# A two-model forward pass on one core: the forget-log sums of the recurrent mixer, with stacked parts and another order

## The reference, cut to what matters

```
q, f, i, g, u = split(rmsnorm(x) @ w_in)
log_f = logaddexp(log(lb), log1p(-lb) + log_sigmoid(f))   # forget logs, (token, channel)
k = (1 - lb) * sigmoid(-f);  v = i
S_t = diag(exp(log_f_t)) S_{t-1} + k_t (outer) v_t
o_t = S_t^T q_t
o = o * rsqrt(mean(o*o) + eps) * norm_g * silu(g)
```

## Time and profile before

| | |
|---|---|
| median of 3 runs | 2926.18 us (2925.79 to 2926.19) |
| the profiled execution's own time | 2925.35 us |
| its span, first to last instruction | 2923.6 us |
| PE busy | 2892.8 us, 99% |
| DVE busy | 2029.5 us, 69% |
| ACT busy | 1297.4 us, 44% |
| POOL busy | 575.4 us, 20% |
| mean granted TensorE clock | 0.998 |

### The profile page before, as it was taken

How to read it: one execution, slowest core, us unless ns; L and a number is a source line. 1 busy time by engine, 2 the same in 40 slices (tenths; PEclk the granted TensorE clock), 3 DMA queues, 4 the chain that set the end, 5 groups by cost and what they waited for, 6 DMA issues and landing times.

```text
span 2923.6 us, 40420 instructions
## 1 busy us (share of the span) xinstructions
PE 2892.8 (99%) x16738; PEld 2501.0 (86%) x16738; DVE 2029.5 (69%) x2542; ACT 1297.4 (44%) x1619; POOL 575.4 (20%) x380
## 2 busy tenths in 40 slices
PE   8999999999999999999999999999999999999998
PEld 6786877868899988888889998899988888889997
DVE  5656556565788884575668887788874665678887
ACT  5545445354534335434543333443346434443332
POOL 0000000000344310200033441343400200034431
PEclk9999999999999999999999999999999999999999
DMA  4121221212233232113222222322332123222222
GB/s 162 44 87 51 101 87 44 89 61 89 99 119 106 101 114 105 35 64 134 91 87 101 101 102 101 108 101 92 111 110 101 43 73 130 80 93 102 101 102 73
DMA packets 41959, 270.10 MB, mean 92 GB/s; under 512 B 5776, under 2 KB 6032, under 8 KB 10672
## 3 DMA queue, kind: packets, MB, share of 16 engines
q1 hardware_dynamic: 41776, 267.52, 25.8%
HBM read 265.33 MB, written 2.10 MB: 91 GB/s over the span
## 4 chain that ended last, share of the span: by engine, by line
PE 89%; DVE 6%; ACT 3%; issue 1%; DVEq 1%; DMA 0%; POOL 0%; SPq 0%; ACTq 0%; POOLq 0%
PE PS L313 27%; PE PS L315 26%; PE PS L314 26%; PE PS L691 1%; PE PS L2426 1%; PE PS L1211 1%; DVE w_lo L287 1%; PE PS L1239 1%; ACT w_hi L279 1%; DVE XT L1724 1%; DVEq L1697 1%; PE PS L750 1%; PE PS L1052 0%; DVE ff_a L1711 0%; PE PS L2406 0%
## 5 line engine op out<-in xcount | busy, mean ns | idle before, releaser
L287 DVE TENSOR_TENSOR w_lo<-w_raw,w_hi 128x2048 fp32r<-128x2048 f32 x167 | 382.6, 2291 | 308.5 <-ACT w_hi L279 307.2
L279 ACT ACTIVATE w_hi<-w_raw 128x2048 fp32r<-128x2048 f32 x169 | 323.2, 1912 | 419.4 <-PE PS L315 419.2
L313 PE MATMUL PS<-uh_b,w_hi 128*128 128x256 f32 (+1 forms) x1096 | 358.9, 327 | 0.0
L315 PE MATMUL PS<-uh_b,w_lo 128*128 128x256 f32 (+1 forms) x1096 | 357.9, 327 | 0.0
L314 PE MATMUL PS<-ul_b,w_hi 128*128 128x256 f32 (+1 forms) x1096 | 357.7, 326 | 0.0
L209 ACT ACTIVATE w_hi<-w_raw 128x1536 fp32r<-128x1536 f32 x72 | 107.3, 1491 | 477.8 <-PE PS L315 477.8
L313 PE MATMUL PS<-uh_a,w_hi 128*128 128x512 f32 (+1 forms) x792 | 288.7, 364 | 1.1 <-DVE ul_a L639 0.7
L314 PE MATMUL PS<-ul_a,w_hi 128*128 128x512 f32 (+1 forms) x792 | 285.5, 360 | 0.0
L315 PE MATMUL PS<-uh_a,w_lo 128*128 128x512 f32 (+1 forms) x792 | 285.5, 360 | 0.0
L313 PE MATMUL PS<-ff_h_hi,w_hi 128*128 128x512 f32 x704 | 278.4, 395 | 5.0 <-DVE XT L1724 4.5
L314 PE MATMUL PS<-ff_h_lo,w_hi 128*128 128x512 f32 x704 | 274.5, 390 | 0.0
(11 more groups left out here) (400 smaller groups left out, 6549.5 us busy)
## 6 DMA issues: line engine op xcount, KB each, us to landing
w_raw<-in_weights SPq DMA_DIRECT2D x241, 1024.0 KB, 4.8
XT<-in_xT SPq DMA_DIRECT2D x8, 256.0 KB, 6.1
mem_raw<-in_mem SPq DMA_DIRECT2D x2, 1024.0 KB, 5.4
out<-XT SPq DMA_DIRECT2D x8, 256.0 KB, 2.0
bands<-in_bands SPq DMA_DIRECT2D x2, 768.0 KB, 6.3
w_raw<-in_weights SPq DMA_DIRECT2D x4, 256.0 KB, 4.7
p_raw<-in_pT SPq DMA_DIRECT2D x2, 512.0 KB, 3.8
lb<-in_lb_logits SPq DMA_DIRECT2D x2, 512.0 KB, 5.7
```

The lines of the kernel that those rows point to most:

```text
L279: act.activation(self.hi[g % 2][:], self.raw[g % 2][:], ACT.Copy).then_inc(self.hi_done.sem, 1)
L287: dve.tensor_tensor(self.lo[g % 2][:], self.raw[g % 2][:], self.hi[g % 2][:], ALU.subtract).then_inc(self.lo_done.sem, 1)
L313: pe.matmul(out, sh, mh, start=first, stop=False, skip_group_check=onto)
L315: return pe.matmul(out, sl, mh, start=False, stop=last, skip_group_check=onto)
```

## The change: what it does

The two parts of the forget logs are no longer two products over 128 tokens. The table `level` has a property: the columns of the tile's first 64 tokens need only logs of the first 64 tokens; those of the last 64 tokens need only logs of the last 64, but for the eighth group, which also needs the sum of all the first 64. So a stationary operand is built for each half of the tile: 64 partitions with the `hi` parts of its 64 tokens and 64 with their `lo` parts. `early` (in `m.LFhi`) is that of the first half, `late` (in `u[1]`) that of the second. The tables are stacked alike. `sums` becomes three matmuls: `late` over 512 columns, `early` over 64 columns of ones, and `early` over 512 columns.

The operands are made in other places: ACT copies half the partitions in the projection (same free size), DVE subtracts into the other half there. After the projection ACT copies the second half's `hi` parts in two pieces (between the table `after` and the queries), and DVE makes their `lo` parts in two pieces. ACT also copies 64 columns of ones. ACT's exponent writes to `m.E` in runs of 64 elements in place of 128. `decays` takes its ones from another tile and now stands between head 0's second and third sums.

```diff
@@ PoolAndStates.scalar
         k.w.wait_used(act, self.proj.g0 + 9)
-        act.activation(uh[:, 6, 0:P], m.after, ACT.Copy).then_inc(self.tables_hi.sem, 1)
+        act.activation(uh[:, 6, 2 * P:2 * P + HALFP], k.ones[:].to_broadcast([P, HALFP]), ACT.Copy)
+        act.activation(uh[:, 6, 0:2 * P], m.after, ACT.Copy).then_inc(self.tables_hi.sem, 1)
+        for a in (0, 2):
+            act.activation(self.u[1][HALFP:P, a:a + 2, :], m.LF[HALFP:P, a:a + 2, :], ACT.Copy).then_inc(self.proj.lf_hi.sem, 1)
         for h in range(HH):
             act.activation(m.Q[:, h, :], k.PS[:, 4 + h, :], ACT.Copy).then_inc(self.proj.qread.sem, 1)
@@ MixerProjection.scalar and .vector
-        act.activation(m.LFhi[:, :, 0:DA], m.LF[:], ACT.Copy).then_inc(self.lf_hi.sem, 1)
+        act.activation(m.LFhi[0:HALFP, :, 0:DA], m.LF[0:HALFP], ACT.Copy).then_inc(self.lf_hi.sem, 1)
...
         w.split_lo(dve, g0 + 7)
+        dve.wait_ge(*self.lf_hi.at(1))
+        dve.tensor_tensor(m.LFhi[HALFP:P, :, 0:DA], m.LF[0:HALFP], m.LFhi[0:HALFP, :, 0:DA], ALU.subtract)
@@ PoolAndStates.vector
-        dve.wait_ge(*self.proj.lf_hi.at(1))
-        k.w.wait_used(dve, self.proj.g0 + 9)
-        dve.tensor_tensor(self.u[1][:, 0:NT, :], m.LF[:], m.LFhi[:, :, 0:DA], ALU.subtract).then_inc(self.lf_lo.sem, 1)
+        for a in (0, 2):
+            dve.wait_ge(*self.proj.lf_hi.at(2 + a // 2))
+            dve.tensor_tensor(self.u[1][0:HALFP, a:a + 2, :], m.LF[HALFP:P, a:a + 2, :], self.u[1][HALFP:P, a:a + 2, :],
+                              ALU.subtract).then_inc(self.lf_lo.sem, 1)
@@ PoolAndStates.tensor
-        pe.wait_ge(*self.lf_lo.at(1))
         for c in range(NT):
+            pe.wait_ge(*self.lf_lo.at(1 + c // 2))
             pe.wait_ge(*self.proj.qread.at(c + 1))
-            pe.matmul(k.PS[:, 4 + c, :], uh[:, 6, 0:P], self.lf_hi_of(c), start=True, stop=False)
-            pe.matmul(k.PS[:, 4 + c, :], uh[:, 6, 0:P], ul[:, c, :], start=False, stop=True).then_inc(self.suffix.sem, 1)
+            early, late = self.parts(c)
+            pe.matmul(k.PS[:, 4 + c, :], uh[:, 6, 0:P], early, start=True, stop=False)
+            pe.matmul(k.PS[:, 4 + c, :], uh[:, 6, P:2 * P], late, start=False, stop=True).then_inc(self.suffix.sem, 1)
@@ Recurrence.scalar
-                act.activation(m.E[(h + 1) % 2][:, :, c * P:(c + 1) * P],
-                               k.PS[:, b:b + 2, :].rearrange("p a (l t) -> p (a l) t", t=P), ACT.Exp).then_inc(self.exped.sem, 1)
+                act.activation(m.E[(h + 1) % 2][:, :, c * P:(c + 1) * P].rearrange("p l (a t) -> p a l t", a=2),
+                               k.PS[:, b:b + 2, :].rearrange("p a (l t) -> p a l t", t=HALFP), ACT.Exp).then_inc(self.exped.sem, 1)
@@ Recurrence.tensor
-            for half in range(2):
-                bank = k.PS[:, 2 * (c % 2) + half, :]
-                pe.matmul(bank, self.states.lf_hi_of(c)[:, h * P:(h + 1) * P], uh[:, 4 + half, :], start=True, stop=False)
-                i = pe.matmul(bank, ul[:, c, h * P:(h + 1) * P], uh[:, 4 + half, :], start=False, stop=True)
-            i.then_inc(self.summed.sem, 1)
+            early, late = (part[:, h * P:(h + 1) * P] for part in self.states.parts(c))
+            first, second = k.PS[:, 2 * (c % 2), :], k.PS[:, 2 * (c % 2) + 1, :]
+            pe.matmul(second, late, uh[:, 5, :], start=True, stop=False)
+            pe.matmul(second[:, LEVELS * HALFP:], early, uh[:, 6, 2 * P:2 * P + HALFP], start=False, stop=True)
+            pe.matmul(first, early, uh[:, 4, :], start=True, stop=True).then_inc(self.summed.sem, 1)
...
-        for c in range(NT):
-            sums(0, c)
+        sums(0, 0)
+        sums(0, 1)
         pe.wait_ge(*self.kcopied.at(1))
         self.states.decays(pe)
+        sums(0, 2)
+        sums(0, 3)
         self.states.states(pe)
```

More of the change, by code:

```diff
@@ L52 @@
 SUMS_BANK = 7
+HALFP = P // 2
 def constants():
@@ L84, in constants @@
     after = (s > t).astype(np.float32)
-    second = np.concatenate([ident, level.reshape(P, -1), after], 1)
+    half = P // 2
+    levels_of = [np.tile(level[a:a + half, :, a:a + half].reshape(half, -1), (2, 1)) for a in (0, half)]
+    after_of = [np.tile(after[a:a + half], (2, 1)) for a in (0, half)]
+    second = np.concatenate([ident] + levels_of + after_of, 1)
     masks = np.concatenate([np.tile(a, (1, NT)) for a in masks + [s == t]], 1).astype(np.uint8)
@@ L1984, in __init__ @@
         self.lf, self.pooled, self.pool_copied = sig("mixer_lf", 1), sig("mixer_pooled", 4), sig("mixer_pool_copied", 4)
-        self.qread, self.hnorm, self.lf_hi = sig("mixer_qread", NT), sig("mixer_hnorm", 1), sig("heads_fa_row", 1)
+        self.qread, self.hnorm, self.lf_hi = sig("mixer_qread", NT), sig("mixer_hnorm", 1), sig("heads_fa_row", 3)
     def sync(self, sp):
@@ L2120, in __init__ @@
         self.k, self.m, self.proj, self.u, self.tables = k, m, proj, u, tables
-        self.tables_hi, self.lf_lo, self.state_read = sig("heads_fa_turned", 2), sig("states_lf_lo", 1), sig("states_state_read", NT - 1)
+        self.tables_hi, self.lf_lo, self.state_read = sig("heads_fa_turned", 2), sig("states_lf_lo", 2), sig("states_state_read", NT - 1)
         self.mapped, self.mapped_read, self.suffix = sig("states_mapped", 4), sig("states_mapped_read", 4), sig("states_suffix", NT)
@@ L2153, in vector, with parts @@
         dve.drain()
-    def lf_hi_of(self, c):
-        return self.m.LFhi[:, c, 0:DA]
+    def parts(self, c):
+        return self.m.LFhi[:, c, 0:DA], self.u[1][:, c, :]
     def take_states(self, dve):
@@ L2172, in tensor @@
     def tensor(self, pe):
-        k, m, (uh, ul) = self.k, self.m, self.u
+        k, m, uh = self.k, self.m, self.u[0]
         for g in range(4):
@@ L2191, in decays @@
                 d = (c - 1) * HH + h
-                i = pe.matmul(k.PS[:, 4, d:d + 1], m.LF[:, c, h * P:(h + 1) * P], m.level[:, LEVELS * P + P - 1:LEVELS * P + P],
-                              start=True, stop=True)
+                i = pe.matmul(k.PS[:, 4, d:d + 1], m.LF[:, c, h * P:(h + 1) * P], k.ones[:], start=True, stop=True)
         i.then_inc(self.dec.sem, 1)
@@ L2387, in tensor @@
     def tensor(self, pe):
-        k, m, right, (uh, ul) = self.k, self.m, self.right, self.u
+        k, m, right, uh = self.k, self.m, self.right, self.u[0]
         def turn_keys(h):
@@ L2874, in second_memory @@
     ub = big + 16 * 1024
-    m.table = mem.put("table2", [P, (LEVELS + 1) * P + P])
+    m.table = mem.put("table2", [P, (LEVELS + 1) * P + 2 * P])
     m.level, m.after = m.table[:, 0:(LEVELS + 1) * P], m.table[:, (LEVELS + 1) * P:]
```

## The result

| | median (lowest to highest) | profiled execution | span | mean granted clock |
|---|---|---|---|---|
| before | 2926.06 us (2925.26 to 2926.29) | 2925.35 us | 2923.6 us | 0.998 |
| after | 2948.72 us (2939.07 to 2951.47) | 2949.45 us | 2947.7 us | 0.99 |

The ratio is 1.0071, 95% interval 1.006 to 1.0082: the changed kernel is slower, by 22.7 us where 6.1 were forecast, and above the range's end of 2935.7. Its runs also spread over 12 us, those of the kernel before over 1.

What follows compares the result with a forecast made beforehand. ACT, then DVE, bound the mixer up to the scores; then PE and DVE take turns. A layer 2.9 - 0.6 + 0.35 + 0.4 = +3.05 us, two +6.1: 2932.3 us, range 2925.0 to 2935.7.

Steps and rivals of the forecast that it cites:

- What bounds the mixer's start: Projection to head 0's scores: the path is ACT without a gap, then DVE; ACT's added 2.25 us are uncovered.
- The small matmul: 64-column matmul in each sum: 0.11 us of PE's path, so a sum falls from 0.92 to 0.57 us.
- ACT's copies: Behind the projection: ones 0.17, wider table 0.11, two log copies 1.98 us; transposes 2.25 us later.
- DVE's two halves: Subtractions of about 1.2 us each behind ACT's pieces, with pooled groups done 1.2 us before the first sum: no cost.
- The decays' move: Decays ahead of head 0's third sum: costs about 1.0 us a layer, from 0 to 1.3.
- Start of the scores: Head 0's scores in each layer start 2.9 us later, from 2.3 to 3.3.
- The two waits: New PE idle time: 2.2 us ahead of the first transposes and 2.6 us ahead of head 0's scores.
- Heads: After the scores' start, a layer: head 0 -0.6 us (-0.3 up to unit 5), head 1 +0.35, head 2 +0.4.
- head 1's contention: POOL starts before DVE's last two multiplications, which take 0.82 and 1.28 us: DVE 1.0 us late, head 1 +0.35.
- TensorE's clock falls in the new idle time: Rival, chance 0.07: one stretch at 1.2 GHz a layer costs 1.9 us, 3.8 on top of the forecast: 2936.1.

Runs made afterwards that it cites:

- e3: The kernel before with four ACT copies of 512 elements (2.1 us, never read) added behind the table copy; 2931.46 us, ratio 1.0017.
- e7: The changed kernel with the second half's hi parts rounded on DVE, not ACT, and the decays back behind head 0's four sums; 2932.00 us, ratio 1.0021.
- e4: The kernel before with only the decays moved, between head 0's second and third sums; 2939.3 us, ratio 1.0042.
- e2: The changed kernel with PE's wait ahead of the transposes filled by eight repeated 512-column suffix matmuls; 2949.12 us, ratio 1.0077.
- e12: The changed kernel with the decays back behind head 0's four sums and both wide matmuls of each sum issued twice; 2935.38 us, ratio 1.0029.
- e6: The changed kernel with both wide matmuls of each sum issued twice (same values); 2936.78 us, ratio 1.0039.
- e13: e9 with matmuls repeated where PE waits: a suffix pair ahead of the transposes and some sums in heads 0 to 2; 2925.33 us, ratio 0.9996.
- e1: The changed kernel with the decays back behind all four sums of head 0; 2937.31 us, ratio 1.004.
- e5: e2 with ten more 512-column matmuls filling PE's wait ahead of head 0's scores; 2937.61 us, ratio 1.0037.
- e9: The changed kernel with tables rounded once, decays back, state copies earlier on DVE and head 1's last two sums among head 0's scores; 2930.39 us, ratio 1.0016.
- e11: The changed kernel with tables rounded once and decays back, but state copies and head 1's last sums left in place; 2937.07 us, ratio 1.0034.

## Why the prediction was wrong

**What bounds the mixer's start: right.** ACT's queue is the path: e3's 2.07 us of delay arrive at the scores as 2.09 and cost 4.7 us in the program.

**The small matmul: right.** In layer 2 of e7, behind it in each sum, the next wide one starts after 0.03 us, and the following sum's first after 0.31 in place of 0.23: 0.11 us together, as taken.

**ACT's copies: nearly right.** The transposes are 2.55 us later, not 2.25. The queries start 2.61 us behind ACT's first instruction, 0.22 before: 2.39 for 2.25, since the copies don't overlap as I had taken (1200.38 + 0.40 ends at 1200.78, the next starts at 1200.80). The other 0.16 are the queries, which took 2.09 to the next instruction for 1.91 before; why is open. DVE's two halves ended ahead of the sums, as said.

**The decays' move: right in the order, wrong in what it brings.** The scores start 1.15 us later (e4) for 1.0 forecast; alone it costs 12.6 us in the program, 24 us of low clock in it.

**Start of the scores: +3.05 (e2, layer 1) for +2.9.** My bounds of 2.3 to 3.3 hold it. The two waits were right as well: 2.20 and 2.67 us for 2.2 and 2.6.

**Heads: direction right in heads 0 and 1.** Head 0 gave -0.23 up to unit 5 (forecast -0.3); head 1's contention is there, as this row set of the changed kernel shows beside the earlier trace rows:

```profile
1247.92 4.91 POOL L2250 TENSOR_TENSOR E<-E,Kf 128x256 f32<-128x256 f32 x6 [17.58 <-ACT E L2263]
...
1248.26 0.67 DVE L2329 TENSOR_TENSOR E<-E,Q 128x256 f32<-128x256 f32 x1 [0.17 <-issue]
1248.85 1.22 DVE L2333 TENSOR_TENSOR E<-E,Q 128x512 f32<-128x512 f32 x1
```

POOL has begun, and the two take 0.67 and 1.22 us in place of 0.43 and 0.69 (0.82 and 1.28 forecast). At full clock (e7) it eats head 0's gain: unit 5 of head 1 stands at +0.02 and +0.03 us from the scores' start against the two layers before. But behind it nothing more is lost, where I had +0.4 for head 2. From the scores' start to the end, e7's second layer takes 0.1 us less than layer 1 before and 0.5 less than layer 2, where I had +0.15 for all heads. So I estimate the schedule's cost at 2 x 3.05 - 0.6 = 5.5 us, for 6.1 forecast, and the changed kernel at full clock at some 2931 us (2929 by the runs' clocks above). That this is so near is in part luck: the start was 0.15 a layer dearer than forecast, and the heads 0.3 to 0.7 cheaper.

**The clock: the step that failed.** I gave "TensorE's clock falls in the new idle time" a chance of 0.07 and 3.8 us. It fell, and holds 23.9 - 5.5 = 18.4 us. Both the chance and the price of that rival were wrong. The chance rested on the lengths of the new waits and on a mean clock of 0.998. The waits came as forecast; that they would leave the clock alone was the error. A mean of almost 1 says that the clock had not fallen, not how near to falling it was. But a wait is only half of it: with the wide sums, e3 (1.94 us) and e12 (2.20) have at most one fall of some 3 us a layer there and e6 (2.20) none, while e13, with the shorter sums and a wait of 0.30, falls for 7. The change did two things at once to the same stretch: it put waits into it, and it took the wide matmuls out of it, and left there the one-column decays, the states and the thin scores. The price rested on the program's first nine matmuls, one stretch with an end soon after the earlier trace rows; its level was read from their spacing, and the clock record itself has 1.00 there. In the mixer the thin products of head 0 follow, and the clock stayed low for 10 to 17 us at a time, and for some 3 twice, 48 in all, at 18.4 / 48 = 0.38 us each (0.5 would be a path that is all PE).

The Trainium skill (TensorE: Matmul & The Clock Gate, Part 1) was weighed in the prediction for its rule that idle time brings the throttled state back. It pointed at the right danger, and I followed the traces' 0.998 instead. The changed kernel agrees, with falls behind waits of 2.19 and 2.67 us. Taken alone the rule is too narrow here: in e13 the clock fell in a stretch whose records have PE busy 4.00 of 4.00 us.

**Where the clock fell.** The profiled executions of all kernels, layer by layer, show four places:
- Within 1.5 us of the transposes' start, where PE had waited 1.94 to 2.20 us for them: layer 1 of the changed kernel, both layers of e1 and e12, layer 2 of e3.
- 12 to 15 us behind the first pooling-map matmul, among decays and states: one layer each of e1, e2, e5, e7, e9, e11 and e13, all with the shorter sums.
- At head 0's scores, or in PE's wait of 0.5 to 2.7 us ahead of them: both layers of the changed kernel, e2 and e4, layer 1 of e11.
- In later heads: the changed kernel, e1, e2, e5, e7, e9 and e11, all with the shorter sums. In e7 layer 1 PE waits 1.00 us there just ahead of the fall; e13 fills these waits and has no fall there.

**What is shown and what is not.** Shown: the time beyond the forecast is spent at the lower clock (48 us of it, none before); more work with later scores is faster where the clock holds (e6); the order of the decays alone, on the kernel before, brings the clock down (e4, 12.6 us); so does the wait ahead of the transposes alone, but for some 3 us in one layer of two (e3); the second and fourth place have falls only with the shorter sums, in e7 with 0.25 us of ACT's delay left. Not shown: whether it is the missing columns that count or the short waits that they leave (0.5 to 1.0 us), since every experiment that put columns back filled waits too. For the second place e13 speaks for the thin work: PE waited 0.30 us at most between the suffix sums and its fall. The parts don't add in both directions: put in one by one, the delay costs 4.7 us (e3), the order 12.6 (e4) and the shorter sums 5.7 (e7, with 0.25 us of delay), 23.0 in all; taken out one by one, the order and the shorter sums give 12 us back each (e1, e6), and both together only 13.3 (e12). Open: why layer 1 falls and layer 2 does not in e7, e9 and e13, with the same code, and why some runs of one kernel fall for longer than others.

## What to carry to other kernels

When an edit takes wide matmuls out of a stretch that also holds waits and thin products, price the clock first: the work removed may have been part of what held it up, and the loss (23 us here) can be twice the whole saving (11 us of PE time at most). Test it by a version that repeats the removed work; if it is faster, the clock is the cause. Then see in its trace which waits the repeats filled, before you put it down to the columns. Shorten such a stretch only together with the waits in it, as e9 and e13 do (and even they do not beat the kernel before), and read the granted clock of each layer by itself.

## What the runs showed of the hardware

- The granted clock fell with PE busy 4.00 of 4.00 us by the records (e13, 1212 to 1216), and did not fall in either mixer of e6 with a wait of 2.20 us; in e12, with the same wait, it fell in both for some 3 us.
- Once down, it stayed at the lower level through thin products with PE busy all of the time (changed kernel, 1228 to 1236 us; e4, 1224 to 1232).
- At the lower level weight loads slow too: in the changed kernel's layer 1 the 16 of the decays took 3.75 us (1.98 before), the 24 of the states 4.55, the last 1 us of it at full clock again (2.88 in e2, all at full clock).
- A 64-column float32r matmul between two wide ones cost 0.11 us of PE's path (e7, layer 2).
- An ACT copy of 1024 elements a partition took no less over 64 partitions than over 128: 2.00 us for two, and 1.08 for one.
